# FFN 2's gate and up projections by blocks with seven products, with one weight sum made in memory, two by VectorE and one by GpSimd

## The reference, cut

```
def swiglu(h, w_gate, w_up, w_down):
    return (jax.nn.silu(h @ w_gate) * (h @ w_up)) @ w_down

for l in range(DEPTH):
    mod = c_act @ ada_w[l] + ada_b[l]
    ...
    h = modulate(rms_norm(x, norm_ffn1[l]), sh1, sc1)
    x = x + 0.5 * g1[:, None, :] * swiglu(h, ffn1_w_gate[l], ffn1_w_up[l], ffn1_w_down[l])
    ...
    x = x + g2[:, None, :] * token_mixing(...)
    h = modulate(rms_norm(x, norm_ffn2[l]), sh3, sc3)
    x = x + 0.5 * g3[:, None, :] * swiglu(h, ffn2_w_gate[l], ffn2_w_up[l], ffn2_w_down[l])
return rms_norm(x, final_norm)
```

## Time and profile before

| | us |
|---|---|
| median of 3 runs | 1163.62 |
| lowest, highest | 1163.49, 1168.38 |
| the profiled execution | 1163.01 |
| its span | 1161.2 |
| TensorE busy | 1145.9 (99%) |
| VectorE busy | 625.5 (54%) |
| ScalarE busy | 451.7 (39%) |
| GpSimd busy | 58.9 (5%) |

### The profile page before, as it was taken

One profiled execution on the slowest core, in us unless ns is written; L12 is line 12 of the kernel. 1 busy time (PEld: TensorE's weight loads), 2 busy tenths in 40 slices (PEclk: granted clock), 3 DMA queues, 4 the chain that ended last, 5 costly groups with the idle time before them and its releaser, 6 DMA issues.

```text
span 1161.2 us, 16214 instructions
## 1 busy us (share of the span) xinstructions
PE 1145.9 (99%) x5730; PEld 969.9 (84%) x5730; DVE 625.5 (54%) x1051; ACT 451.7 (39%) x709; POOL 58.9 (5%) x86
## 2 busy tenths in 40 slices
PE   8899999999999999999999999999999999999997
PEld 7788888888888998888888888899888888888887
DVE  5766666666555666776565566756433333333332
ACT  5233332332222357665555566434322222222232
POOL 3301000000000000010001010000000000000000
PEclk9999999999999999999999999999999999999999
DMA  9567566556555423343343442341333333333332
GB/s 312 162 219 243 181 218 204 174 184 211 172 172 167 110 63 102 91 125 86 90 120 96 111 117 72 91 139 37 97 98 101 90 98 101 90 93 94 99 113 74
DMA packets 221149, 151.45 MB, mean 130 GB/s; under 512 B 5078, under 2 KB 202916, under 8 KB 221108
## 3 DMA queue, kind: packets, MB, share of 16 engines
q1 hardware_dynamic: 217108, 138.76, 39.8%
q0 software_dynamic: 3280, 9.79, 3.2%
q10 hardware_dynamic: 720, 2.36, 0.6%
HBM read 148.73 MB, written 4.52 MB: 132 GB/s over the span
## 4 chain that ended last, share of the span: by engine, by line
PE 91%; DVE 2%; SPq 2%; issue 1%; DMA 1%; ACT 1%; POOL 0%; DVEq 0%; POOLq 0%; ACTq 0%
PE bank L1492 28%; PE bank L1494 28%; PE bank L1493 28%; PE bank L1827 2%; PE bank L1820 1%; SPq L446 1%; PE bank L1843 1%; PE bank L1815 1%; PE bank L1842 1%; DMA raw<-in_ffn_w_gate_dram 1%; SPq L465 1%; DMA adas<-in_ada_w_dram 1%; SPq L459 0%; DVE hL L1010 0%; DVE tmp L1005 0%
## 5 line engine op out<-in xcount | busy, mean ns | idle before, releaser
L1492 PE MATMUL bank<-hH,wH 128*128 128x512 f32 (+1 forms) x1072 | 413.2, 385 | 3.6 <-DVE hL L1010 3.1
L1494 PE MATMUL bank<-hH,wL 128*128 128x512 f32 (+1 forms) x1072 | 409.0, 382 | 0.0
L1493 PE MATMUL bank<-hL,wH 128*128 128x512 f32 (+1 forms) x1072 | 408.8, 381 | 0.0
L617 ACT ACTIVATE wH<-raw 128x1024 fp32r<-128x1024 f32 (+1 forms) x169 | 176.2, 1042 | 500.2 <-PE bank L1494 500.2
L944 DVE TENSOR_TENSOR wL<-raw,wH 128x1024 fp32r<-128x1024 f32 (+1 forms) x169 | 203.4, 1204 | 280.3 <-ACT wH L617 279.7
L1492 PEld LDWEIGHTS bank<-hH,wH 128*128 128x128 f32 x1072 | 201.6, 188 | 44.4 <-issue 5.1
L1494 PEld LDWEIGHTS bank<-hH,wL 128*128 128x128 f32 x1072 | 201.5, 188 | 39.1
L1493 PEld LDWEIGHTS bank<-hL,wH 128*128 128x128 f32 x1072 | 201.8, 188 | 37.7
L1492 PE MATMUL bank<-actH,wH 128*128 128x512 f32 (+1 forms) x332 | 126.9, 382 | 0.0
L1494 PE MATMUL bank<-actH,wL 128*128 128x512 f32 (+1 forms) x332 | 126.6, 381 | 0.0
L1493 PE MATMUL bank<-actL,wH 128*128 128x512 f32 (+1 forms) x332 | 126.6, 381 | 0.0
(11 more groups left out here) (204 smaller groups left out, 1188.6 us busy)
## 6 DMA issues: line engine op xcount, KB each, us to landing
adaw<-in_ada_w_dram SPq DMA_DIRECT2D x28, 1024.0 KB, 6.0
raw<-in_ffn_w_gate_dram SPq DMA_DIRECT2D x43, 512.0 KB, 3.8
raw<-in_ffn_w_up_dram SPq DMA_DIRECT2D x43, 512.0 KB, 3.8
raw<-in_mix_w_in_dram SPq DMA_DIRECT2D x41, 512.0 KB, 3.8
raw<-in_ffn_w_down_dram SPq DMA_DIRECT2D x32, 512.0 KB, 3.7
adas<-in_ada_w_dram SPq DMA_DIRECT2D x16, 512.0 KB, 8.2
raw<-in_ffn_w_down_dram SPq DMA_DIRECT2D x16, 384.0 KB, 3.4
raw<-in_mix_w_out_dram SPq DMA_DIRECT2D x8, 512.0 KB, 3.7
```

Of the source, the lines that this page charges most:

```text
L617: nc.scalar.activation(wH[s][:, :n * P], raw[s][:, :n * P], ACT.Copy).then_inc(hi_done, 1)
L1492: T.matmul(o, a[0], b[0], start=start, stop=False)
L1493: T.matmul(o, a[0], b[1], start=False, stop=False)
L1494: return T.matmul(o, a[1], b[0], start=False, stop=stop)
```

## The change

FFN 2's weights are taken as blocks of two. A pair of D_FF tiles i and i + 11, for gate and for up, has four weight blocks (two halves of the 1024 contraction rows, two tiles), and the tokens have four blocks (two halves of the contraction rows, two halves of the tokens). A 2 x 2 product of blocks takes eight block products; the change uses a scheme with seven, of sums of weight blocks and sums of token blocks, and further sums of the products. One product here is gate and up together: 2 x 4 x 3 = 24 matmuls of 256 columns.

- The first two pairs (`DIRECT`) stay as units: four in `to_ffn` and four after it. Nine pairs (`N_TWOS`) follow, 63 products in the order `ORDER_P`, written out and not in a loop. Weights in the loop have three slots (`w_slot`), raw tiles four (`raw_slot`: `raw` and two act tiles not yet in use).
- Weight sums. The sum for product 5 is made in memory, `wsum_d`: GpSimd issues 8 transfers that copy half of the rows (during FFN 1's down) and 8 that add the other half (between the bias transfers of the mixing stage), each of 128 x 1408 elements in pieces of 128 elements. From it VectorE makes the sums for products 6 and 3 by one addition each (`next_r`), and GpSimd that for product 7 (L780 of the kernel after). A pair loads five raw tiles of 512 KB, each as two transfers.
- Token sums: GpSimd adds `hH` and `hL` for four blocks (`whole`), VectorE makes four sums of them (`token_sums`), ScalarE and VectorE their high and low parts (`t_high`, `t_low`).
- Product sums: ScalarE copies two of a pair's products from PSUM (`kept`), VectorE makes seven sums (`block`). Silu, multiplication and the parts of act follow on them (`gates`, `multiply`, `act_high`, `act_low`).
- `down` of FFN 2 has its first two units' weights in `tH`, `tL`; its first unit waits for 16 act tiles, the second for all 22. SyncE loads the weights of down after the last low part of the loop.

The diff, cut to its core:

```diff
+    ORDER_P = (1, 2, 5, 6, 7, 3, 4)
+    B_P = {1: 4, 2: 7, 5: 5, 6: 6, 7: 0, 3: 1, 4: 2}
+    N_BL, N_TWOS = len(ORDER_P), HF - DIRECT
+    N_PROD = N_BL * N_TWOS
+    LOADS = (1, 2, 5, 7, 4)
...
+        def sp_ffn_by_blocks(sp):
...
+            sp.wait_ge(w_summed, 16 * 4 * SUM_ROWS)
+            for l in range(N_LOAD * N_TWOS):
...
+                if l < 2:
+                    sp.wait_ge(lo_done, U_DN2 - 1 + l + FREE)
+                elif l == 2:
+                    sp.wait_ge(t_lo, 3)
+                elif l >= RAW_SLOTS:
+                    t0, p0 = (l - RAW_SLOTS) // N_LOAD, LOADS[(l - RAW_SLOTS) % N_LOAD]
+                    if p0 in (1, 2):
+                        sp.wait_ge(r_made, 2 * t0 + p0)
+                    if p0 == 1:
+                        sp.wait_ge(q_made, t0 + 1)
+                    elif p0 != 2:
+                        sp.wait_ge(w_lo, N_BL * t0 + ORDER_P.index(3 if p0 == 5 else p0) + 1)
+                for m in range(2):
...
+                    sp.dma_start(raw_slot(l)[:, m, :].rearrange("p (k n) -> p k n", k=DT // 2), src
+                                 ).then_inc(w_in[l % RAW_SLOTS], 16)
+            for i in range(DT // 2):
+                for k in range(6):
...
+                    if i == 0 and k < 2:
+                        sp.wait_ge(w_lo, N_PROD)
...
+            def weight_sum(step):
...
+                if kind < 2:
+                    pool.dma_start(to, w[0, row:row + P, HF * P:], max_dma_last_dim=PACKET).then_inc(w_summed, 16)
+                else:
+                    pool.wait_ge(w_summed, 16 * 2 * SUM_ROWS)
+                    pool.dma_start(to, w[0, D // 2 + row:D // 2 + row + P, HF * P:], accum_op=ALU.add,
+                                   max_dma_last_dim=PACKET).then_inc(w_summed, 16)
...
+                if n == 4:
+                    pool.wait_ge(hL_done, 5 * DT)
+                    for q in range(4):
+                        whole(q)
+                    for t in range(N_TWOS):
...
+                        nc.gpsimd.tensor_tensor(raw_slot(l7), raw_slot(l7), raw_slot(l1), ALU.add).then_inc(q_made, 1)
...
+            def w_high(n):
+                l, p = load_of(n), ORDER_P[n % N_BL]
+                if p in (6, 3):
+                    act.wait_ge(r_made, 2 * (n // N_BL) + 1 + (p == 3))
+                elif p == 7:
+                    act.wait_ge(q_made, n // N_BL + 1)
+                else:
+                    act.wait_ge(w_in[l % RAW_SLOTS], 32 * (l // RAW_SLOTS + 1))
+                if n < 2:
+                    act.wait_ge(unit_done, U_DN2 - 1 + n)
+                elif n >= W_SLOTS:
+                    act.wait_ge(p_done, n - W_SLOTS + 1)
+                nc.scalar.activation(by_two(w_slot(n)[0]), raw_slot(l), ACT.Copy).then_inc(w_hi, 1)
...
+                t_low(6, 1)
+                t_low(7, 2)
+                t_low(4, 3)
+                w_low(0)
+                w_low(1)
+                t_low(5, 4)
+                product(1, 1)
+                lo(1, 1)
+                for t in range(N_TWOS):
+                    two_by_blocks(t)
...
+                for n in range(N_PROD):
...
+                    pe.wait_ge(w_lo, n + 1)
+                    wh, wl = w_slot(n)
+                    h, l = moving(p)
+                    for m in range(2):
+                        for k in range(DT // 2):
+                            cols = slice((m * DT // 2 + k) * P, (m * DT // 2 + k + 1) * P)
+                            ins = three(bank[:, B_P[p], HALF[m]], (wh[:, cols], wl[:, cols]), (h[:, k, :], l[:, k, :]),
+                                        k == 0, k == DT // 2 - 1)
+                    ins.then_inc(p_done, 1)
...
-                        pe.wait_ge(actL_done[n], k0 + cnt + START)
+                        pe.wait_ge(actL_done[n], (k0 + cnt if n == 0 else FT if k0 else 2 * cnt) + START)
```

More of the change, by code:

```diff
@@ L348, in hybrid_block @@
         out_sent = sem("out_sent")
+        w_summed = sem("w_summed")
+        w_in = [sem(f"w_in{q}") for q in range(RAW_SLOTS)]
+        r_made = sem("r_made")
+        q_made = sem("q_made")
+        w_hi = sem("w_hi")
+        w_lo = sem("w_lo")
+        p_done = sem("p_done")
+        h_whole = sem("h_whole")
+        t_sum = sem("t_sum")
+        t_hi = sem("t_hi")
+        t_lo = sem("t_lo")
+        kept = sem("kept")
+        c_made = sem("c_made")
+        gated = sem("gated")
+        multiplied = sem("multiplied")
         def head_rows(h):
@@ new lines, in two_by_blocks @@
+            def two_by_blocks(t):
+                for at in range(N_BL):
+                    n = N_BL * t + at
+                    if n + 2 < N_PROD:
+                        w_high(n + 2)
+                    else:
+                        k = n + 2 - N_PROD
+                        act.wait_ge(p_done, N_PROD - N_BL + 4 + k)
+                        prep_home(U_DN2 + k, U_DN2)
+                    if t and at == 1:
+                        gates(t - 1, 1)
+                    if t and at in (2, 3):
+                        act_high(t - 1, at - 2)
+                    if at == 1:
+                        act.wait_ge(p_done, n)
+                        if t:
+                            act.wait_ge(multiplied, 2 * t - 1)
+                        nc.scalar.activation(K_P1, bank[:, B_P[1], :], ACT.Copy).then_inc(kept, 1)
+                    if at == 3:
+                        act.wait_ge(p_done, n)
+                        if t:
+                            act.wait_ge(multiplied, 2 * t)
+                        nc.scalar.activation(K_P5, bank[:, B_P[5], :], ACT.Copy).then_inc(kept, 1)
+                    if at == 6:
+                        gates(t, 0)
@@ new lines, in multiply, with two_by_blocks @@
+            def multiply(t, j):
+                dve.wait_ge(gated, 2 * t + 1 + j)
+                dve.wait_ge(c_made, 7 * t + (5, 7)[j])
+                s, c = by_halves(sg[:, j, :]), of_up((c1, c2)[j])
+                if j == 0:
+                    V.tensor_tensor(s, s, c, ALU.mult).then_inc(multiplied, 1)
+                else:
+                    V.scalar_tensor_tensor(out=s, in0=c, scalar=-1.0, in1=s, op0=ALU.mult, op1=ALU.mult).then_inc(multiplied, 1)
+            def two_by_blocks(t):
+                for at in range(N_BL):
+                    n = N_BL * t + at
+                    if n + 2 < N_PROD:
+                        w_low(n + 2)
+                    else:
+                        prep_home(U_DN2 + n + 2 - N_PROD)
+                    if at < 2:
+                        next_r(t, at)
+                    if t and at == 0:
+                        block(t - 1, 6)
+                        multiply(t - 1, 0)
+                    if t and at == 2:
+                        multiply(t - 1, 1)
+                        act_low(t - 1, 0)
+                    if t and at == 3:
+                        act_low(t - 1, 1)
+                    for step in {4: (0, 1), 5: (2, 3), 6: (4, 5)}[at] if at >= 4 else ():
+                        block(t, step)
```

255 lines of the change are left out of this document (235 added, 20 removed).

## The result

The kernel after takes 1158.22 us (median of 8 runs, 1155.71 to 1161.91) against 1163.55 for the kernel before: a ratio of 0.9943, 95% interval 0.9928 to 0.9958. (The ratios in this document are of means; two of the eight executions before took 1168.4 and 1168.6, so the ratio of the medians is nearer to 1, 0.9954.) It is faster, by 5.3 us, and 3.3 us slower than forecast.

A forecast was written before the change was run, and what follows sets the result against it. TensorE's matmul columns in FFN 2's gate and up were taken as the bound; -14.6 + 2.4 + 2.3 + 0.85 + 0.3 = -8.75 us gave 1154.3 on the profiled scale, 1154.9 as median, range 1150 to 1163.

The forecast's parts named there:

- What bounds the kernel: FFN 2's gate and up, 217.62 us, is bound by TensorE's matmul columns; time saved there counts if other engines keep up.
- TensorE's saving, 14.6: In FFN 2's gate and up, 36 units at 195.9 us become 63 products at 181.3; bounds 13.1 and 16.1.
- Start, 2.4: At the block loop's start TensorE waits 1.6 us, then 0.8 at product 3, for queued work; bounds 0.8 and 4.5.
- Sharing, 0.85: GpSimd's add holds VectorE 1.7 us a block, free in the loop, adding 0.85 us in the first block.
- the row of 0.43 us: Trace meeting at 33.80: VectorE's pair of passes held 0.43 us by GpSimd; basis for 1.7 us per add.
- End, 2.3: At the loop's end the first down unit waits 0.4 us for weights, the second 1.9 for act tiles; bounds 0.5 and 4.5.
- Transfers, 0: Block loop loads: transfer share rises from 0.34 to about 0.46, but loads land in time; 0 us, bound +2.
- sums in memory, 0.3: 16 GpSimd transfers of 704 KB pass beside loads, in FFN 1's down and mixing; 0.3 us, bounds 0 and +5.
- VectorE as the bound: Rival in the block loop: meetings cost 3.4 us instead of 1.7, over the spare; 1164, no change; chance 0.12.
- The starved addition: Rival: VectorE's two-input passes delay GpSimd's add until product 4's high part waits; at 7.5 us a pass 1172; chance 0.07.
- Late loads and fetches: Two rivals: loads landing in 6 us, 1159, chance 0.07; TensorE waiting for instruction fetches, 1167, chance 0.05.
- More room at the ends: Rival: queues have more room at both loop ends, which cost 1 us, not 5; 1151; chance 0.10.

The follow-up runs named there:

- e11: Against after: VectorE, not GpSimd, makes the sum for product 7, placed in its idle time, and w_down's first load is early; 1151.87 us, ratio 0.9890.
- e4: Against after: GpSimd adds only one column of each half for product 7's weight sum, so results are wrong; 1154.14 us, ratio 0.9910.
- e5: Against after: the 16 memory sums and their wait left out, product 5 reading weights directly, so results are wrong; 1157.53 us, ratio 0.9950.
- repeat: The kernel after measured again, unchanged; 1157.35 us, ratio 0.9936 to before.
- e6: Against after: last raw load put into the raw tile freed one load later, so w_down's first load is issued earlier; 1155.55 us, ratio 0.9922.
- e13: The kernel of e11 measured again; 1151.74 us, ratio 0.9892 to before.

## Why the prediction was right, and where it was off

- **What bounds the kernel**: right. The stage stayed TensorE's; the stretch fell by 7.7 us, against 8.75 in the sum. Part of that nearness is luck: the saving came out 1.0 larger than its term, and start and end together 0.5 smaller (without the addition), against 2.2 more for sharing.
- **TensorE's saving, 14.6**: 15.6. The stage of e11 is 204.43 us; less four direct units of 21.79 in all, waits of 2.27 and slow steps of 0.15, it leaves 180.2 for 1512 matmuls, 0.1192 each where the earlier trace rows gave 0.1199. The rule that the prediction took from the Trainium skill (TensorE: Matmul & The Clock Gate, "Back-to-back issue gap"), 0.109 and a saving of 21.4, does not agree with this trace; that section gives the rule for an isolated matmul only, and its 0.131 us for 512 columns in a stream with weight loads does not agree with the 0.2267 here either.
- **Start, 2.4**: 2.27 where GpSimd adds next to nothing (1.58 and 0.69 for the forecast 1.6 and 0.8). The count of the queues was right, with one slip: the listed items add up to 7.1 us and not 7.3, which would be a first wait of 1.3. The sign given for it, two waits of 1 to 2 us near 835 to 845, is not what came: after has one of 3.05 there, and without the addition they are 1.58 and 0.69.
- **Sharing, 0.85**: the step that failed. The size of a meeting was about right: 1.63 us at 838.74 against 1.7. Its place was not: at the start I charged half of it, and it fell whole on TensorE's path (1.5 to 1.7), 0.6 to 0.8 more came at the first down unit, and the wait of 3.05 was followed by the fall of the clock (1.4), for which the sum had no term. In the loop itself it cost nothing, as said, except for stray waits of 0.2 to 0.7 in some profiles. Together 2.7 to 3.0 us by the stretch of e4, 3.2 to 4.1 by the medians. The Trainium skill (SBUF — State Buffer, "Terms") says that the lock is held for the full instruction. The trace agrees for passes with two SBUF inputs on both sides. I had weighed that rule, priced it at 2 us more at the two ends, and taken the row of 0.43 us instead, which belongs to a GpSimd pass with one input tensor. With the rule the forecast would have been 1156.9. In the row of 0.43 us (33.67) VectorE's pair ends at 35.52, before GpSimd's pass at 35.86, so it wasn't held for the whole of it: this case shows both.
- **End, 2.3**: 0.43 and 1.54 without the addition, 1.20 and 1.55 in after. The mechanism was the load, not only the count: with w_down's load early both go.
- **Transfers, 0, and sums in memory, 0.3**: no effect on the time that can be measured (e5). A transfer of 704 KB to memory lands in 7.7 us, and the loads of 384 KB take 4.2 us with the sums and 3.4 without.
- **Rivals.** VectorE as the bound: not in after, but the reserve is a matter of place. The starved addition: no, it took 2.38 to 2.8 us. Late loads and fetches: none waited for in the loop, and w_down's first was issued late, not slow; fetches rose from 25 to 38. More room at the ends: no, less.
- **Still open**: why the median lies further off than the trace. The profiled execution of after, 1155.71, is 1.4 us above the forecast on its scale (1154.3); the other 1.9 of the 3.3 lie between it and the median. By the profiled executions after gains 7.7 us on the stretch, by the medians 5.3 (after) and 6.8 (repeat). The clock is part of it: the executions of after have a mean granted clock of 0.992 to 0.996, the longest (1161.91) 0.992; of the 52 of before that stand beside the experiments the eight above 1166 us have 0.994, and the rest 0.995 to 0.999. Where the clock fell in executions without a profile isn't known, nor whether the change makes it fall more often.

## What to carry over

An engine's idle share says whether there is room for an operation; the rows of its queue say where. The same nine additions cost 13 us between a producer and its consumer, and nothing in a gap of 1.05 us that was already there. GpSimd's additions in SBUF are not free work beside a busy VectorE: where one meets the path, look at its whole duration, cut it, or move it to the engine that would have been held. And at the end of a stage, one late load at the head of an in-order queue delays all that stands behind it.

## What the runs showed of the hardware

- GpSimd and VectorE exclude each other for whole instructions when both read two SBUF tensors: VectorE's 0.68 us became 2.31 beside an addition of 2.38; GpSimd's sum in four pieces took 5.22, and VectorE's passes beside it 0.90, 1.56 and 1.63. A VectorE pass with a PSUM input kept its 0.68.
- The granted clock after the start wait fell to the 1.2 GHz level for some 3.4 us in after (0.77 on average over 842.53 to 850.00), and in e5 and e6, each behind a wait of TensorE of 3.05 to 3.44 us. In the repeat it stayed at the full level behind one of 3.32, and it never fell behind the waits of up to 2.3 us in the other kernels.

```profile
843.40:850.00 6.60, 5.87 (x47) 5.72 (x48) 5.41 (x6) 4.03 (x5) 0.00 (x0) 1.00 0.31 90
```

That is the repeat's row for the same time, at 1.00. What decides between the two is open. At the start of the program the level also falls, for 6.8 us in e11 and for 10.2 in e13, which took 4.8 us longer.
